# A hybrid decoder step on one core: small remainders of the experts as float32 blocks on four column groups, with earlier first weights and spread loads

## The chip, the cores and the metric

One core of a Trainium2 chip runs the whole step. The metric is the device time of one execution in microseconds; the kernel before takes 2387.33 us, the median of 3 runs.

## What is computed

One decoder layer over 2048 prompt rows and 8 decode rows, float32 throughout, width 1024. The last part is a mixture of experts: each row picks one of 4 groups and 2 of the 8 experts in it, so 2056 rows make 4112 assignments over 32 experts. Cut to what matters here:

```python
s = einsum(q, k) + bias            # three dilations (1, 4, 16), window 128 keys each, softmax, combined
x = x + gt1 * (concat([att, conv]) @ w_out)
h = rmsnorm(x, g_n2) * (1 + sc2) + sh2
eid, wts = route(h)                # group by argmax, then top 2 of its 8 experts
y[row] = sum over its 2 experts of wts * ((silu(h @ w1[e]) * (h @ w3[e])) @ w2[e])
x = x + gt2 * y                    # then one last rmsnorm
```

w1 (gate) and w3 (up) are 1024x512, w2 (down) is 512x1024, for each of the 32 experts: 6 MiB an expert.

## The kernel before

The step runs as stages one after another, each with its own buffers and with a barrier of all engines between them: setup and input projection; prompt attention; the decode rows' mixers; output projection and routing; experts; combining and the last norm. Engines are ordered by semaphores written out by hand; each engine runs its own program in its own order.

**Attention** (`prompt_attention`) walks 48 blocks of 128 queries: 16 for dilation 1, 16 for dilation 4, 16 for dilation 16. A block sees its own keys and mostly the block before (a wide block), or its own alone (narrow: all of dilation 16, and the first of each residue). SP loads at the start the bias bands of all three branches (lines 849 to 855), then QN, KN and VN (256 KB each) for the blocks to come (line 881 on), two slots for QN and KN. VectorE first waits for all three bias loads. ScalarE issues between its exponentials the loads for the stage behind: dec_q (2 MiB) at block 0, the three of dec_k (2 MiB each) at blocks 0 to 2, the three of dec_v at 12 to 14 (lines 1021 to 1029).

**Routing** (`output_projection_and_routing`) works tile by tile on 16 tiles of 128 rows and the decode rows: projection, norm, h2 stored to DRAM, router, rank of each row in its expert. POOL scatters each row's number into slot_tokens at expert x CAP + rank (line 1639). Counts of rows per expert come last, from one matmul and a VectorE copy.

**Experts** (`experts`, line 2040 on). `tables` (VectorE, lines 2096 to 2104) makes for each expert its number of 128-row blocks (at least one) and the first and the end of its run of blocks. Each engine reads these bounds into registers and loops over experts and blocks. For a block b of expert e:

- POOL loads 128 indices (IDX, line 2177) and gathers the rows (XG, line 2165), one block ahead: it waits until TensorE has transposed the block before (x_turned), then for its own gather.
- TensorE transposes XG into XP (line 2298). ScalarE rounds it to the fast float32r format (XH), VectorE takes the rest (XL).
- The weights are split likewise: ScalarE writes HI (line 2210, two halves a weight), VectorE LO (line 2256). A product is then three passes of float32r matmuls: HI with XH, HI with XL, LO with XH. Gate gives AE, up gives BE, 24 matmuls of 512 columns each (line 2309); ScalarE makes the silu SE from AE (line 2220), VectorE G = SE x BE in two halves (line 2267); TensorE turns G (line 2304), ScalarE and VectorE make GH and GL (lines 2224, 2271), and down gives YP, 24 matmuls (line 2314). ScalarE copies YP to YE in two halves (line 2230) and stores it (line 2232).
- In an expert's last block ScalarE and VectorE split the next expert's weights as well: gate after the silu, up after XH, down after the store (for VectorE all three after XL). SP loads a half of a raw weight (W1E, W3E, W2E; 1 MiB) as soon as VectorE has ended the same half of the expert before (lines 2149 to 2154).

`destinations` (VectorE, lines 2116 to 2120, in expert 0's first block) works out where each row's two results lie, for the last stage's gathers.

Of the kernel before, what the change touches and what calls it, by code (L numbers as in the profile page):

```python
# [9 lines left out]
F32R = mybir.dt.float32r  # L10
# [7 lines left out]
P = 128  # L18
# [26 lines left out]
MAXBLK = NEXP + (2 * ROWS) // P + 1  # L45
VEC = 384
# [71 lines left out]
def decoder_step(nc, t, const_at, stop_after=99):  # L118

    with ExitStack() as whole:  # L120
# [30 lines left out]
        with ExitStack() as both:  # L151
# [6 lines left out]
            if stop_after >= 3:  # L158
                decode_mixers(nc, t, scratch, const, const_at, state)
        if stop_after >= 4:  # L160
            state["token"] = persistent("token", [P, ALLT], I32)
            for name in ("rank", "expert", "weight"):
                state[name] = persistent(name, [P, ALLT, 2])
            state["count"] = persistent("count", [P, NEXP])
            state["lower"] = persistent("lower", [P, NEXP * NEXP])
            output_projection_and_routing(nc, t, scratch, const, const_at, state)
        late = whole.enter_context(ExitStack())
        if stop_after >= 5:
            for name, shape in (("gate6", [P, 2, D]), ("gf6", [P, D])):
                state[name] = persistent(name, shape)  # L170
            lasting = stage_semaphores(nc, late)
            state["mods6_in"] = lasting("mods6_in")
            state["blocks"] = persistent("blocks", [P, 2 * NEXP], I32)
# [567 lines left out]
def prompt_attention(nc, t, dr, const, state):  # L741
# [66 lines left out]
    with ExitStack() as ctx:  # L808
# [24 lines left out]
        bias_in = sem("bias_in")  # L833
# [12 lines left out]

        with nc.Block() as block:
            @block.sync
            def _(sp):
                for b in range(3):  # L850

                    v = dr["band"][b]
                    wide = 2 if b < 2 else 1
                    skew = bass.AP(v.tensor, v.offset + P - 1 + (2 - wide) * P, [[HEADS * VEC - 1, P], [VEC, HEADS], [1, wide * P]])
                    sp.dma_start(BIAS[b][:], skew).then_inc(bias_in, 16)

# [47 lines left out]
                for q in range(2):  # L904
                    load_qk(0, q, 0, None)
                step(0, 0)
# [31 lines left out]
            def _(dve):  # L938
                dve.wait_ge(bias_in, 48)
# [31 lines left out]
                def round_(g):  # L971
                    maxima(g)
                    if g.at or not g.fixed:
                        take_probs(g, 1)
                        take_columns(g, 1)

# [6 lines left out]
            def _(act):  # L983
# [37 lines left out]
                def ahead(g):  # L1021
                    dq_in, dk_in, dv_in = state["dec_in"]
                    if g == 0:
                        act.dma_start(state["dec_q"][:], dr["dec"][0:1].to_broadcast([P, DEC, DATT])).then_inc(dq_in, 16)
                    for at, cache, dst, come in ((0, t["cache_k"], state["dec_k"], dk_in), (3, t["cache_v"], state["dec_v"], dv_in)):
                        for n, dil in enumerate(DILATIONS):
                            if g == 4 * at + n:
# [429 lines left out]
def output_projection_and_routing(nc, t, dr, const, const_at, state):  # L1457
# [27 lines left out]
    with ExitStack() as ctx:  # L1485
# [9 lines left out]
        WO, WOH, WOL = sb("WO", [P, KD, D]), sb("WO_H", [P, KD, D], F32R), sb("WO_L", [P, KD, D], F32R)  # L1495
# [19 lines left out]
        NOROWS = sb("NOROWS", [P, D])  # L1515
        norows_set, norows_out, lower_in = sem("norows_set"), sem("norows_out"), sem("lower_in")
# [18 lines left out]
        with nc.Block() as block:  # L1535
            @block.sync
            def _(sp):
# [10 lines left out]

                def round_(i):
# [209 lines left out]
            def _(dve):  # L1759
# [141 lines left out]

                dve.wait_ge(mods_in, 16 * 11)
# [47 lines left out]
                nc.vector.tensor_copy(state["count"][:], NP_[:]).then_inc(count_ready, 1)  # L1950

# [98 lines left out]
def experts(nc, t, dr, const, state):  # L2050
# [4 lines left out]

    with ExitStack() as ctx:
# [3 lines left out]
        def ps(name, shape):  # L2060
# [4 lines left out]
        W1, W3, W2 = sb("W1E", [P, KD, DEXP]), sb("W3E", [P, KD, DEXP]), sb("W2E", [P, KF, D])  # L2065
        fetching = sem("fetching")
        IDX, XG, XH, XL = sb("IDX", [P, 1], I32), sb("XG", [P, D]), sb("XH", [P, KD, P], F32R), sb("XL", [P, KD, P], F32R)
        S, G, GH, GL, Y = sb("SE", [P, DEXP]), sb("GE5", [P, DEXP]), sb("GH", [P, KF, P], F32R), sb("GL", [P, KF, P], F32R), sb("YE", [P, D])
        HI = [sb(f"HI{n}", [P, KD * DEXP], F32R) for n in range(3)]
# [5 lines left out]
        w1_in, w3_in, w2_in = ([sem(f"{x}_w_in{half}") for half in range(2)] for x in ("gate", "up", "down"))  # L2075
# [3 lines left out]
            sem("y_taken"), sem("yrows_out"))  # L2079
        table = state["blocks"]  # L2080
        CMP, NBLK, LOW, START, END = sb("CMP", [P, NEXP, 16]), sb("NBLK", [P, NEXP]), sb("LOW", [P, NEXP, NEXP]), sb("START", [P, NEXP]), sb("END", [P, NEXP])
        SEL, BASE = sb("SEL", [P, ALLT * 2, NEXP]), sb("BASE", [P, ALLT * 2])
        step, table_ready = sem("table_step"), sem("table_ready")

# [438 lines left out]
```

## Time and profile before

| | |
|---|---|
| runs (3) | 2387.33 us median, 2385.10 to 2388.75 |
| profiled execution | 2385.13 us, of which the span 2383.6 us |
| busy in the span | TensorE 86%, its weight loads 70%, VectorE 68%, ScalarE 48%, POOL 24% |
| attention's first load to decode's first | 582.1 to 958.3 us |
| experts' stage | from 1360.2 to about 2285 us |
| mean granted clock | 0.936 of full |

In the rows, PE is TensorE's matmuls and PEld its weight loads, DVE is VectorE, ACT ScalarE, POOL GpSimd, and SPq or ACTq a DMA issue on that engine's queue. L2309 is line 2309 of the kernel before. A float32 matmul is recorded twice, a float32r one once. "Idle" is the engine's idle time before the group, and behind the arrow stands what ended it. A clock of 1.00 is 2.4 GHz, 0.50 is 1.2 GHz.

### The profile page before, as it was taken

What the parts mean: (1) busy time and instruction counts of PE and PEld (TensorE: products, weight loads), DVE (VectorE), ACT (ScalarE), POOL (GpSimd) and SP (SyncE); (2) the same over time, 40 slices, a digit from 0 to 9 for tenths busy, and PEclk for the clock granted to TensorE, in tenths of its full rate; (3) what the DMA queues carried; (4) which work ended last, traced back from release to release, by engine and by line L of the source; (5) the groups of instructions that cost most, each with busy time, mean ns of one, the idle gap of its engine ahead of it and who ended that gap; (6) DMA issues with size and microseconds to landing.
All of it is one profiled execution on the core that took longest, in us unless ns stands there. A gap on an engine that the chain in (4) does not pass through costs nothing. (4 is left out here: it accounts for less than half of the span.)

```text
span 2383.6 us, 37684 instructions
## 1 busy us (share of the span) xinstructions
PE 2059.1 (86%) x12062; PEld 1671.2 (70%) x12063; DVE 1627.6 (68%) x3132; ACT 1154.4 (48%) x2115; POOL 560.6 (24%) x560
## 2 busy tenths in 40 slices
PE   5999999996999997539999489999999999999910
PEld 3788888885777775328888368888888888888810
DVE  2568888887666666739998558664635666467868
ACT  2311111122777786024444158665546666457833
POOL 1024444440111111203555210000000000000066
PEclk7999999998999999659999689999999999999965
DMA  8755555554855454855776269876655878677977
GB/s 270 260 209 194 195 194 194 197 196 136 287 183 187 134 169 126 285 197 191 255 256 234 73 243 397 319 279 257 242 198 198 330 271 303 235 260 294 380 280 294
DMA packets 221091, 560.26 MB, mean 235 GB/s; under 512 B 27885, under 2 KB 41541, under 8 KB 219848
## 3 DMA queue, kind: packets, MB, share of 16 engines
q1 hardware_dynamic: 178544, 436.70, 52.3%
q0 software_dynamic: 26144, 79.49, 9.1%
q10 hardware_dynamic: 16320, 43.01, 4.8%
q8 instruction: 46, 0.75, 0.1%
q14 instruction: 37, 0.30, 0.0%
HBM read 460.66 MB, written 171.04 MB: 265 GB/s over the span
## 5 line engine op out<-in xcount | busy, mean ns | idle before, releaser
L591 DVE SCALAR_TENSOR_TENSOR ARENA<-ARENA,TAPW 128x512 f32<-128x512 f32 (+3 forms) x493 | 293.3, 674 | 0.0
L417 POOL TENSOR_TENSOR MS<-SSQ,K 128x1 f32<-128x1 f32 x17 | 172.3, 10136 | 289.8 <-ACT H L460 289.8
L2267 DVE TENSOR_TENSOR GE<-SE,BE 128x256 f32<-128x256 f32 x98 | 36.9, 418 | 272.0 <-PE BE L2309 269.6
L710 PE MATMUL PJ<-WIN_H,HTH 128*128 128x512 f32 x680 | 172.4, 396 | 15.1 <-ACT HTH L466 11.7
L492 ACT ACTIVATE ARENA<-PJ 128x512 f32<-128x512 f32 x51 | 30.5, 600 | 293.6 <-PE PJ L718 293.6
L1017 ACT ACTIVATE PR<-SBX,NM 128x256 f32<-128x256 f32 (+1 forms) x384 | 171.9, 456 | 1.0 <-PE TB L1104 0.8
L714 PE MATMUL PJ<-WIN_H,HTL 128*128 128x512 f32 x680 | 170.4, 393 | 0.0
L718 PE MATMUL PJ<-WIN_L,HTH 128*128 128x512 f32 x680 | 168.1, 389 | 0.0
L710 PEld LDWEIGHTS PJ<-WIN_H,HTH 128*128 128x128 f32 x680 | 127.3, 189 | 45.8 <-ACT HTH L466 15.9
L2165 POOL DMA_INDIRECT XG<-h_rows,IDX x50 | 50.4, 1008 | 455.3 <-PE XP L2298 439.9
L714 PEld LDWEIGHTS PJ<-WIN_H,HTL 128*128 128x128 f32 x680 | 129.7, 191 | 27.4
L718 PEld LDWEIGHTS PJ<-WIN_L,HTH 128*128 128x128 f32 x680 | 127.6, 188 | 26.5
L2256 DVE TENSOR_TENSOR LO<-W1E,HI 128x2048 fp32r<-128x2048 f32 x64 | 143.6, 2283 | 3.4 <-ACT HI L2210 3.4
L2256 DVE TENSOR_TENSOR LO<-W3E,HI 128x2048 fp32r<-128x2048 f32 x64 | 143.6, 2284 | 0.6 <-ACT HI L2210 0.6
L2256 DVE TENSOR_TENSOR LO<-W2E,HI 128x2048 fp32r<-128x2048 f32 x64 | 143.6, 2285 | 0.0
L2210 ACT CAST HI<-W1E 128x2048 fp32r<-128x2048 f32 x64 | 120.1, 1902 | 36.2 <-DMA W1E<-in_w_expert_gate 35.7
L952 DVE CUSTOM_DVE_ANT_0 SBX<-S,BIAS 128x256 f32<-128x256 f32 (+1 forms) x384 | 117.5, 362 | 22.7 <-issue 22.7
L2210 ACT CAST HI<-W2E 128x2048 fp32r<-128x2048 f32 x64 | 120.5, 1911 | 25.6 <-ACT YE L2230 14.9
L2210 ACT CAST HI<-W3E 128x2048 fp32r<-128x2048 f32 x64 | 120.1, 1918 | 1.7 <-DMA W3E<-in_w_expert_up 1.5
L2177 POOL DMA_DIRECT2D IDX<-slot_tokens x48 | 27.5, 573 | 355.8 <-issue 245.0
L2314 PE MATMUL YP<-HI,GH 128*128 128x512 f32 x392 | 104.6, 409 | 4.2 <-ACT GH L2224 3.2
L1127 PE MATMUL OT<-PTS,VN 128*64 128x128 f32 x1200 | 90.8, 284 | 19.2 <-DVE PTS L965 19.2
(310 smaller groups left out, 4717.7 us busy)
## 6 DMA issues: line engine op xcount, KB each, us to landing
W1E<-in_w_expert_gate SPq DMA_DIRECT2D x64, 1024.0 KB, 8.3
W3E<-in_w_expert_up SPq DMA_DIRECT2D x64, 1024.0 KB
W2E<-in_w_expert_down SPq DMA_DIRECT2D x64, 1024.0 KB, 11.6
expert_rows<-YE ACTq DMA_DIRECT2D x49, 512.0 KB, 5.8
expert_rows<-NOROWS POOLq DMA_DIRECT2D x11, 1536.0 KB, 11.7
WAD<-in_w_ada SPq DMA_DIRECT2D x16, 1024.0 KB, 7.0
X<-in_x_prompt SPq DMA_DIRECT2D x31, 512.0 KB
QN<-q_rows SPq DMA_DIRECT2D x48, 256.0 KB, 3.1
```

Source lines behind the costliest of these rows:

```text
L417: pool.tensor_tensor(MS[:], SSQ[:], const("eps"), ALU.add).then_inc(ms_ready, 1)
L591: ins = nc.vector.scalar_tensor_tensor(out=out, in0=src, scalar=tap, in1=out, op0=ALU.mult, op1=ALU.add)
L710: nc.tensor.matmul(PJ[:, n], HTH[:, k], WH[:, n, k], start=k == 0, stop=False)
L714: nc.tensor.matmul(PJ[:, n], HTL[:, k], WH[:, n, k], start=False, stop=False)
L718: mm = nc.tensor.matmul(PJ[:, n], HTH[:, k], WL[:, n, k], start=False, stop=k == KD - 1)
L952: nc.vector.tensor_tensor_reduce(SBX[hh][:, h, 0:wide], SP_[hh][:, at_bank(h), 0:wide], bias, 1.0, -3e38, ALU.add, ALU.max, ml[:, head:hea ...
L1017: ins = nc.scalar.activation(PR[hh][:, h, 0:w], SBX[hh][:, h, 0:w], ACT.Exp, bias=NM[:, head:head + 1], scale=1.0, accum_out=ML[g.q][:, HE ...
L1127: mm = nc.tensor.matmul(OT[s * DH:(s + 1) * DH, pair], VN[(q - nk + 1 + k) % 4][:, head * DH:(head + 1) * DH], PTS[:, u, n], start=k == 0, ...
L2165: pool.indirect_dma_start(XG[:], None, dr["h2"], bass.IndirectOffsetOnAxis(ap=IDX[:].bitcast(U32), axis=0)).then_inc(x_in, 16)
L2210: nc.scalar.copy(HI[n][:, cols], raw[n][:, cols]).then_inc(hi_ready[n], 1)
L2256: nc.vector.tensor_tensor(LO[n][:, cols], raw[n][:, cols], HI[n][:, cols], ALU.subtract).then_inc(lo_ready[n], 1)
L2314: mm = nc.tensor.matmul(YP[:, half * 512:half * 512 + 512], g[:, k], w[2][:, k * D + half * 512:k * D + half * 512 + 512], start=first and ...
```

## The change

**Experts.** The first of an expert's rows may form a small block of up to 32 rows (`SMALL_ROWS`), when count - 128 x FULL is 1 to 32, where FULL is the number of full blocks, at least one; such an expert has one full block less than before. Experts 0 and 31 always have a small block. The 32 experts become runs that begin with a small block. A small block uses the raw float32 weights: its rows are the stationary operand, 32 columns wide, and a weight's columns go in four quarters to four groups of 32 rows of the output.

**First weights.** W1E and W3E share a buffer (WIDE) with the projection's raw w_out, and expert 0's gate and up are requested in the routing stage's last rounds; its down is requested after the first gather. The table is made at the end of the routing stage; the destinations are worked out at the end of VectorE's program in the experts' stage.

**Attention.** QN and KN go first, then the first branch's bias; ScalarE issues the other two at blocks 1 and 2. dec_k goes out at blocks 3, 13 and 15, dec_v at 32, 34 and 44, dec_q at 46.

The diff, cut to its core:

```diff
+SMALL_ROWS = 32
 # attention
-                dve.wait_ge(bias_in, 48)
+                dve.wait_ge(bias_in[0], 16)
...
                 for q in range(2):
                     load_qk(0, q, 0, None)
+                load_bias(sp, 0)
...
+                    if g in (1, 2):
+                        load_bias(act, g)
-                    if g == 0:
+                    if g == 46:
                         act.dma_start(state["dec_q"][:], ...)
 # routing: last rounds of SP
+                def first_expert(name, n):
+                    sp.wait_ge(w_lo_ready, KD)
...
+                    if isinstance(i, int) and i == TILES - 2:
+                        first_expert("w_expert_gate", 0)
+                    if isinstance(i, int) and i == TILES - 1:
+                        first_expert("w_expert_up", 1)
 # routing: VectorE, after the counts (each operation waits for the one before)
+                def experts_table(dve):
+                    then(nc.vector.tensor_scalar(FULL[:], count[:], 1.0 / P, (P - T - 0.5) / P - 0.5, ALU.mult, ALU.add))
+                    then(nc.vector.tensor_scalar(FULL[:], FULL[:], 8388608.0, None, ALU.add))
+                    then(nc.vector.tensor_scalar(FULL[:], FULL[:], -8388608.0, 1.0, ALU.add, ALU.max))
+                    then(stt(SMALL1[:], FULL[:], float(P), count[:], ALU.mult, ALU.is_lt))
+                    for e in (0, NEXP - 1):
+                        then(nc.vector.tensor_scalar(SMALL1[:, e:e + 1], SMALL1[:, e:e + 1], 1.0, None, ALU.max))
+                    below(RUN, SMALL1)
+                    below(FROM, FULL)
...
 # experts: SP
+                sp.wait_ge(x_in, 16)
+                for half in range(2):
+                    sp.dma_start(half_of(W2[:], half), half_of(w2[0], half)).then_inc(w2_in[half], 16)
                 with sp.Fori(1, NEXP) as e:
                     split = sp.snap(e * 2)
+                    sp.wait_ge(sy_done, entry(sp, 4, e, 1, LAST))
...
 # experts: POOL
+                def fetch_small(e, n):
+                    pool.wait_ge(sx_turned, n + 1)
+                    pool.dma_start(IDXS[:], dr["slot"][ds(slot, T), :]).then_inc(sidx_in, 16)
+                    pool.wait_ge(sidx_in, n * 16 + 16)
+                    pool.indirect_dma_start(XGS[:], None, dr["h2"], ...).then_inc(sx_in, 16)
...
+                with pool.Fori(0, number) as g:
+                    head, behind = run(pool, g)
+                    fetch_small(behind, g + 1)
+                    with pool.Fori(pool.snap(head + 1), pool.snap(behind + 1)) as e:
+                        ...
 # experts: ScalarE
+                def small(e, n, meanwhile=None):
+                    act.wait_ge(sx_turned, n + 2)
+                    nc.scalar.copy(XS[:], XPS).then_inc(sx_ready, 1)
+                    act.wait_ge(sa_done, n + 1)
+                    nc.scalar.activation(SS[:], APS, ACT.Silu).then_inc(ss_ready, 1)
+                    act.wait_ge(sg_turned, n + 1)
+                    nc.scalar.copy(GTS[:].rearrange("p k t -> p (k t)"), GPS).then_inc(sgt_ready, 1)
+                    act.wait_ge(sy_out, n * 64 + 64)
+                    act.wait_ge(sy_done, n + 1)
+                    nc.scalar.copy(YS[:], YPS).then_inc(sy_taken, 1)
+                    for q in range(4):
+                        act.dma_start(dr["y"][ds(row, T), cols], YS[q * T:(q + 1) * T]).then_inc(sy_out, 16)
...
+                    with act.Fori(head, behind) as e:
+                        upper(2, e)
+                        first, last = first_and_last(act, e)
...
+                        block_(last, g + 1, lambda n: upper(n, e + 1))
+                    small(behind, g + 1)
 # experts: VectorE has the same loops
+                def small(n):
+                    dve.wait_ge(ss_ready, n + 1)
+                    dve.wait_ge(sb_done, n + 1)
+                    nc.vector.tensor_tensor(GS[:], SS[:], BPS, ALU.mult).then_inc(sg_ready, 1)
 # experts: TensorE
+                def on_groups(out, x, w, ks):
+                    width = w.shape[2] // 4
+                    for k in range(ks):
+                        for q in range(4):
+                            mm = nc.tensor.matmul(out[q * T:(q + 1) * T], x[:, k], w[:, k, q * width:(q + 1) * width], start=k == 0, stop=k == ks - 1)
+                def small(e, n, meanwhile=None):
+                    pe.wait_ge(sx_in, n * 16 + 16)
+                    for k in range(KD):
+                        mm = nc.tensor.transpose(XPS[:, k], XGS[:, k * P:(k + 1) * P], const("ident")[0:T, 0:T])
+                    pe.wait_ge(sx_ready, n + 1)
+                    on_groups(APS, XS, W1, KD).then_inc(sa_done, 1)
+                    on_groups(BPS, XS, W3, KD).then_inc(sb_done, 1)
+                    pe.wait_ge(sg_ready, n + 1)
+                    nc.tensor.transpose(GPS, GS[:], const("ident")).then_inc(sg_turned, 1)
+                    pe.wait_ge(sgt_ready, n + 1)
+                    on_groups(YPS, GTS, W2[:], KF).then_inc(sy_done, 1)
```

In the loops over a run's experts upper(0) and upper(1) of the next expert (ScalarE) and lower(0), lower(1) (VectorE) stay in an expert's last block; upper(2) and lower(2) stand at the start of the expert itself, behind a small block where there is one. TensorE's small block waits for both halves of each raw weight.

## Rows read from the trace of the kernel before

In a row of a stretch the engines stand in the order PE, PEld, DVE, ACT, POOL (busy us and instructions), then the granted clock, the DMA engines' busy share and GB/s; with one line alone, PE and PEld only.

**Rows 1.** Busy time by engine in the experts' stage: window, length, engines, granted clock, DMA, GB/s.

```profile
1360.00:2285.00 925.00, 888.44 (x4124) 728.40 (x4124) 570.47 (x450) 583.27 (x535) 83.78 (x105) 0.98 0.74 277
```

**Rows 2.** The page's groups (busy, mean ns, idle, releaser) and its DMA issues.

```profile
L2267 DVE TENSOR_TENSOR GE<-SE,BE 128x256 f32<-128x256 f32 x98 | 36.9, 418 | 272.0 <-PE BE L2309 269.6
...
expert_rows<-YE ACTq DMA_DIRECT2D x49, 512.0 KB, 5.8
```

**Rows 3.** Timeline of TensorE: start, length; the first group of each block.

```profile
1403.69 1.98 PE L2309 MATMUL AE<-HI,XH 128*128 128x512 f32 x8
1421.72 1.98 PE L2309 MATMUL AE<-HI,XH 128*128 128x512 f32 x8
...
1513.49 1.98 PE L2309 MATMUL AE<-HI,XH 128*128 128x512 f32 x8
```

**Rows 4.** Timeline of ScalarE and VectorE at a handover, and the copies GH by line.

```profile
1421.92 0.59 ACT L2230 COPY YE<-YP 128x512 f32<-128x512 f32 x1 [0.27 <-PE YP L2314]
...
1423.03 4.49 DVE L2256 TENSOR_TENSOR LO<-W3E,HI 128x2048 fp32r<-128x2048 f32 x2
1423.08 3.73 ACT L2210 CAST HI<-W2E 128x2048 fp32r<-128x2048 f32 x2 [0.57 <-ACT YE L2230]
...
L2224 ACT CAST GH<-GP 128x256 fp32r<-128x256 f32 x86 | 31.5, 372 | 121.9 <-PE GP L2304 119.3
```

**Rows 5.** Line 1414 alone in two stretches (two clocks), and line 1448 in the timeline.

```profile
971.30:975.20 3.90, 3.64 (x64) 2.98 (x64) 0.50 0.75 117
978.20:979.60 1.40, 1.08 (x32) 0.81 (x32) 1.00 0.88 322
...
1003.79 5.36 PE L1448 MATMUL OD<-dec_v,PTD 128*32 128x512 f32 x48
```

**Rows 6.** Timeline of TensorE's weight loads in attention.

```profile
646.81 0.42 PEld L1127 LDWEIGHTS OT<-PTS,VN 128*64 128x64 f32 x8 [0.17 <-issue]
```

**Rows 7.** Timeline of POOL in one block, and DMA issues with median time to landing.

```profile
1416.73 0.98 POOL L2165 DMA_INDIRECT XG<-h_rows,IDX  x1 [10.30 <-PE XP L2298]
1423.60 0.57 POOL L2177 DMA_DIRECT2D IDX<-slot_tokens  x1 [5.89 <-issue]
...
W1E<-in_w_expert_gate SPq DMA_DIRECT2D x64, 1024.0 KB, 8.3
...
IDX<-slot_tokens POOLq DMA_DIRECT2D x49, 0.5 KB, 4.9
```

**Rows 8.** Timeline over the end of routing and expert 0's first block.

```profile
1353.29 0.85 POOL L1639 DMA_INDIRECT slot_tokens<-TOK,SLOTP  x1 [0.30 <-issue]
...
1360.29 0.69 DVE L2096 TENSOR_TENSOR CMP<-count,K 128x512 f32<-128x512 f32 x1 [10.47 <-PEq L191]
...
1361.95 1.23 DVE L2100 TENSOR_TENSOR LOW<-lower,NBLK 128x1024 f32<-128x1024 f32 x1
...
1378.51 3.75 PE L2309 MATMUL AE<-HI,XH 128*128 128x512 f32 x8 [1.10 <-ACT XH L2204]
...
1396.04 0.69 PE L2304 MATMUL GP<-K,GE 128*128 128x128 f32 x2 [3.40 <-DVE GE L2267]
...
1397.24 2.98 PE L2314 MATMUL YP<-HI,GH 128*128 128x512 f32 x8
```

**Rows 9.** Timeline at attention's start, QN's landing there, and one QN slot later.

```profile
582.14 2.61 SPq L855 DMA_DIRECT2D BIAS<-band_rows  x3
...
593.17 1.12 PE L1060 MATMUL XPA<-K,QN 128*128 128x128 f32 x4 [20.76 <-DMA QN<-q_rows]
...
597.80 0.06 DVE L948 MEMSET PAUSE<- 128x1 f32 x1 [18.62 <-PE S L1089]
...
QN<-q_rows SPq DMA_DIRECT2D x3, 256.0 KB, 6.7
...
888.69 0.33 SPq L881 DMA_DIRECT2D QN<-q_rows  x1
...
898.97 0.32 PE L1060 MATMUL XPA<-K,QN 128*128 128x128 f32 x1
```

More of the change, by code:

```diff
@@ L159, in decoder_step @@
                 decode_mixers(nc, t, scratch, const, const_at, state)
+        late = whole.enter_context(ExitStack())
         if stop_after >= 4:
+            state["wide"] = persistent("WIDE", [P, KD * D])
+            lasting = stage_semaphores(nc, late)
+            state["first_in"] = [[lasting(f"{x}_w_in{half}") for half in range(2)] for x in ("gate", "up")]
             state["token"] = persistent("token", [P, ALLT], I32)
@@ L2130, in first_and_last, with runs, run @@
             return first, engine.snap(end - 1)
-        raw = [w[:].rearrange("p k n -> p (k n)") for w in (W1, W3, W2)]
+        def runs(engine):
+            return entry(engine, 4, LAST, 1, LAST)
+        def run(engine, g):
+            return entry(engine, 0, g, 0, LAST - 1), entry(engine, 0, g + 1, 1, LAST)
+        raw = [w.rearrange("p k n -> p (k n)") for w in (W1, W3, W2[:])]
         come = (w1_in, w3_in, w2_in)
@@ L2161, in _, with place @@
             def _(pool):
+                def place(value, rows):
+                    return nc.s_assert_within(pool.snap(value), 0, NEXP * CAP - rows,
+                                              skip_runtime_bounds_check_because="an expert's blocks stay inside its CAP slots")
                 def gather(b):
@@ L2316, in into_rows @@
                     return mm
-                pe.wait_ge(table_ready, 1)
-                pe.wait_ge(x_in, 16)
-                turn_x(range(KD)).then_inc(x_turned, 1)
-                with pe.Fori(0, NEXP) as e:
+                def on_groups(out, x, w, ks):
+                    width = w.shape[2] // 4
+                    for k in range(ks):
+                        for q in range(4):
+                            mm = nc.tensor.matmul(out[q * T:(q + 1) * T], x[:, k], w[:, k, q * width:(q + 1) * width],
+                                                  start=k == 0, stop=k == ks - 1)
+                    return mm
@@ L2359, in combine_and_normalise, with first_rows @@
+                def first_rows():
+                    pe.wait_ge(x_in, 16)
+                    turn_x(range(KD)).then_inc(x_turned, 1)
+                small(0, 0, first_rows)
+                number = runs(pe)
+                with pe.Fori(0, number) as g:
+                    head, behind = run(pe, g)
+                    with pe.Fori(head, behind) as e:
+                        expert(e, g + 1)
+                    small(behind, g + 1)
+                expert(LAST, number + 1)
 def combine_and_normalise(nc, t, dr, const, state):
```

320 lines of the change are left out of this document (197 added, 123 removed).

## The prediction

> **What bounds the kernel now.** I read the stretches of the stages first, then the page's costliest groups, then the timeline where one expert's block hands over to the next. In the experts' stage TensorE is busy 888 of 925 us at a clock of 0.98 of full [rows 1], and VectorE stands 272 us before the product that follows BE, released by TensorE [rows 2]: the stage is as long as TensorE's list of blocks. The timeline gives the price of a block: 1403.69 to 1421.72 is 18.03 us, and 1421.72 to 1513.49 is five blocks of experts with one block each, 18.35 us a block [rows 3]; the 0.3 us more is a weak pull of the weights' loads (6 MiB for each expert). The page stores 49 blocks [rows 2]. So a removed block is worth 18.0 us, and what is added between two blocks costs in full what TensorE cannot overlap.
>
> How many blocks go is in the inputs. The reference's own router on its inputs gives the 32 experts 141, 101, 85, 64, 72, 120, 134, 183, 89, 212, 168, 139, 141, 348, 138, 107, 83, 208, 134, 111, 74, 135, 143, 242, 167, 130, 59, 123, 83, 50, 62 and 66 rows. Rounded up to 128 that is 49 blocks, as the trace has. By the new rule (a remainder of 1 to 32 rows is small) 40 full blocks are left: experts 0, 6, 11, 12, 14, 18, 21, 22 and 25 lose one each. Ten small blocks run: these nine, and one without rows for expert 31, which the code forces.
>
> **A small block, step by step**, on the handover at 1421.5, where TensorE begins the weight loads of the next AE (0.2 ahead of the row at 1421.72).
> - Eight transposes of 32 rows: 1.0 us, to 1422.6. Their rows were gathered long before.
> - ScalarE copies them out (XS). It is in order behind YE (ends 1422.5) and the store, and came free at 1423.08 [rows 4]; a 128x256 copy from PSUM takes 0.37 [rows 4], so TensorE resumes at 1423.6.
> - Gate and up: per weight 32 matmuls of 128x32 weights by 128 columns in float32, in four column groups, each recorded twice. That very shape is in the trace: 32 records in 1.08 us at full clock, 64 in 3.64 at half clock [rows 5]. So 64 records take about 1.9, two weights 3.7: to 1427.3. The silu and its table load lie beside the second.
> - The product on VectorE: that engine is in LO of W3E from 1423.03 for 4.49, to 1427.5 [rows 4]. A tie with the matmuls. A 128x128 product is under the 0.42 of 128x256 [rows 2]; I take 0.3: 1427.9.
> - Transpose, copy to GTS, semaphores: 0.7, to 1428.6.
> - Down: 16 matmuls of 256 columns. The nearest row is 24 of 512 columns in the same groups, 5.36 us [rows 5], so 16/24 x 1/2 of it: 1.8, to 1430.4.
>
> That is 8.9 us. The PE array changes between full width and groups four times. **The row**: between full-width and 64-column matmuls the weight loads pause 0.17 us [rows 6]; two of the four changes lie beside a wait, so 0.3. The Trainium skill (TensorEngine Tiling (Array Packing), Key Properties) says that changing the tiling mode drains the engine. By a full drain of some 0.27 us at each of four changes, an estimate from that page and this kernel's matmul length, ten small blocks would cost 8 us more than I count; the row says less, and I go by the row. I add 0.8 for register loads, loop ends and branches on three engines, which no row shows by themselves (bounds 0 and 3), and 0.5 for the next gather (first rival). **A small block costs 10.5 us**, between 8.9 and 14.
>
> ScalarE then stores four pieces (some 0.4 each) and splits W2E, 3.7 [rows 4], to about 1436.5, VectorE ends its LO by 1441; the full block that began at 1430.7 wants them at 1443.5. Covered; without that cover each small block would cost up to 2.5 more. Eight experts (6 to 25 above) thus give 8 x (18.0 - 10.5) = 60.2 us, expert 31 costs 10.5.
>
> **Expert 0 and the stage's start.** Before: stage start 1360.3, expert 1 at 1421.7, 61.4 us, of which the first block took 25 (1378.51 to 1403.69) because its G came late from VectorE, which was at LO of W2E and the destinations (3.4 us of idle TensorE), and then ran its YP at a lower clock (2.98 us for eight) [rows 8]. After, counted from the start: small index load (4.9 to land [rows 7]) and gather, 12; index and gather of the 128 rows behind them, 20 (a gather lands 6.9 after its issue [rows 7]); only then is W2E requested, and its second half lands some 8.3 later [rows 7], 28.3, so that is what the small block's last matmuls wait for; then 2 us and one full block of 18: 48.9. Gain 12.5. Against it, the table moves ahead of the barrier, into the tail of the routing stage, and grows: 7 operations of 128x1024 at 1.23 and some 14 of 32 columns or fewer, which by the line through 0.69 (512 columns) and 1.23 (1024) take about 0.2 with their semaphore, 11.7 us [rows 8]. VectorE ended at 1360.29 - 10.47 = 1349.8 and would now end at 1361.5, while the barrier followed the last scatter (1353.29, landed some 3 later) by about 3. The start moves from 1360.3 to 1364.7, **4.4 us later**. Net 8.1. The early loads of gate and up are 4 MiB on SP behind that stage's last x2 and h2 traffic; SP has nothing late behind them, cost 0. The destinations, four operations, move to VectorE's end, beside the last YP, its copy and store: 0, and a few us if they outlast those.
>
> **Attention.** SP issued the three BIAS loads first at 582.14, the first transposes came at 593.17, released by QN, and VectorE started at 597.80, 18.6 idle [rows 9]. With QN and KN ahead, TensorE starts some 6 earlier; BIAS of branch 0 lands around 592, just when the scores are done. I take 5.5 (bounds 3 and 7). The spread loads: beside them a QN took 6.7 to land [rows 9], but a QN slot is loaded at 888.69 and used again two short blocks on, at 898.97 [rows 9]: slack 10, cost 0. The last one, dec_q at block 46, ends some 8 us before the next stage starts; bound 2.
>
> **Sum**: 60.2 - 10.5 + 8.1 + 5.5 = 63.3 off the profiled execution's 2385.1 (span 2383.6, 1.5 around it) is 2321.8. The median of the runs is 2387.3, 2.2 above that execution: **2324**.
>
> **Rivals.**
> - *The gather becomes the wait.* POOL now fetches the next small block's rows (index, wait, gather) before the next full block's index and gather. From the small transposes at 1422.7: 4.9 + 1 + 0.5 + 4.9 + 1, and 6.9 to land: 1441.9, and TensorE wants it some 11 us into the block, 1441.7. A tie; I counted 0.5. If index loads land 1 us later each, beside three weights in flight, 2 us more at eight experts: 2340. Chance 0.2.
> - *Weights too late.* SP waits for the small block before it requests the next expert's weights, all at once at 1430.4, where they went out from 1421 on. W1E's second half lands at 1438.7, and ScalarE splits it before it copies GH, wanted at 1442.6. It fits by 2 us; if the landing is 12, some 5 us at eight experts: 2364. Chance 0.1.
> - *Slower: the small block runs at half clock.* The place is the holes of 1.0, 0.6 and 0.5 us inside it. The trace has the fall: after 3.4 us without work the next eight matmuls took 2.98 for 1.98 [rows 8]. At half clock gate and up take 7.3 for 3.7, down 3.6 for 1.8, transposes 1.1 more, the block behind 1.4 more: 18.1 for each small block, and 2392 in all. It decides from 17.5 us per small block (63.3 / 9 above 10.5). Against it: around 978 TensorE worked 1.08 us of a 1.40 us stretch on this very shape, and the granted clock there was 1.00 [rows 5]. Chance 0.04. The Trainium skill (TensorE: Matmul & The Clock Gate, What's actually happening) has activity release the throttle and idleness bring it back; that fits this row.
> - *The groups run one after another here*: 3.4 and 1.8 become four times as much, 24 us per small block: 2445. The rows of that shape speak against it. Chance 0.02.
> - *Cheaper than counted*: 9 us per small block, a shorter start: 2306. Chance 0.1. That the blocks do not go is excluded by the counts, unless the rule is not what I read: 0.01.
>
> **Numbers.** Forecast 2324 with 0.53, own range 2310 to 2336. 8 in 10 reaches over the gather's case and the first part of the weights' case: 2302 to 2356. A measurement here tells 0.2%, 5 us, from no change. Faster 0.93, same 0.02 (half clock in part), slower 0.05.
>
> **What would show it.** Forty stores of YE and ten of each small tile; full blocks 18.0 apart, 28.5 where a small one lies between. In a small block: TensorE idle before gate on ScalarE's copy, before the transpose on VectorE's product, with LO of W3E ended just before. Expert 1 starting 49 us into the stage, the stage's start at 1359 (4.4 later, 5.5 earlier), VectorE's first maximum near 592. Wrong if idle time before the XG transposes exceeds 1 us per small expert, if eight matmuls behind a small block take over 2.5, or if gate and up take more than 5.

## The result, and the profile after

The changed kernel takes 2371.23 us (median of 6 runs, 2364.32 to 2377.85), the kernel before on the same chip 2388.04 (6 runs). The ratio is 0.9931, 95% interval 0.9913 to 0.9950: faster by 17 us, where 63 were forecast. 2324 was predicted, and the range ended at 2356. The profiled execution took 2364.32 us, its span 2362.8.

The blocks go as forecast. These are issues on the page of the changed kernel (tile, queue, count, KB each, median us to landing), against 49 in [rows 2]; each small block stores four pieces of YS:

```profile
expert_rows<-YE ACTq DMA_DIRECT2D x40, 512.0 KB, 5.3
...
expert_rows<-YS ACTq DMA_DIRECT2D x40, 32.0 KB
```

And yet the run of blocks got no shorter. Busy time by engine from the first matmul of expert 1's block to that of the last block, in the kernel before and then in the changed one (columns as in [rows 1]):

```profile
1421.72:2254.82 833.10, 828.95 (x3865) 680.20 (x3864) 525.70 (x411) 547.45 (x502) 70.91 (x91) 1.00 0.76 283
```

```profile
1399.37:2233.88 834.51, 778.95 (x4714) 621.22 (x4713) 511.75 (x382) 471.78 (x445) 79.94 (x92) 0.98 0.75 279
```

Eight full blocks fewer lie in this stretch and nine small ones more. It lasts 1.4 us longer, and TensorE, busy 829 of 833 us before, now stands 56 us. All that the change gained lies outside it. By the two traces: attention begins 4.1 us earlier (the setup before it is the same code; over this study's traces the start moved between 577.6 and 583.3), attention and the decode stage are 8.3 shorter from their first load to the projection's first matmul, projection and routing are 4.9 longer, the stretch from the experts' first index load to expert 1 is 14.9 shorter. That sums to 4.1 + 8.3 - 4.9 + 14.9 - 1.4 = 21.0, and the two profiled executions differ by 20.8. Two of these terms are larger in this pair than on the mean. The changed kernel's profiled execution is the fastest of its six. And the stretch from attention's first load to the projection took 474.5 to 477.7 us in the three traces with the old attention code, and 469.4 to 475.8 in the eleven with the new one, of which this is the shortest.

Two things fill the stretch. **First, full blocks are slower where nothing waits.** TensorE's timeline (start, length), one group of eight matmuls to the next, first before:

```profile
1657.85 1.98 PE L2309 MATMUL AE<-HI,XH 128*128 128x512 f32 x8
1659.66 1.98 PE L2309 MATMUL AE<-HI,XL 128*128 128x512 f32 x8
...
1668.74 0.82 PE L2298 MATMUL XP<-K,XG 128*128 128x128 f32 x6
...
1670.31 2.12 PE L2314 MATMUL YP<-HI,GH 128*128 128x512 f32 x8
```

and after:

```profile
1564.98 2.03 PE L2440 MATMUL AE<-HI,XH 128*128 128x512 f32 x8
1566.85 2.03 PE L2440 MATMUL AE<-HI,XL 128*128 128x512 f32 x8
...
1576.18 0.82 PE L2429 MATMUL XP<-K,XG 128*128 128x128 f32 x6
...
1577.92 2.09 PE L2445 MATMUL YP<-HI,GH 128*128 128x512 f32 x8
...
1583.59 2.03 PE L2440 MATMUL AE<-HI,XH 128*128 128x512 f32 x8
```

Eight wide matmuls (128x128 weights by 512 columns) take 1.87 us and not 1.81, and from the XG transposes to YP it is 1.74 and not 1.57. A block takes 18.61 us (1564.98 to 1583.59) against 18.04. **Second, a small block costs 13.5 us** on the mean of the eight inside the loop, not 10.5. (This is the time from the AE of the full block ahead of it to the AE behind it, less one full block of 18.61.) The one at expert 6, TensorE and then ScalarE:

```profile
1493.63 2.02 PE L2445 MATMUL YP<-LO,GH 128*128 128x512 f32 x8
1495.58 0.68 PE L2466 MATMUL XP<-K,XGS 32*128 32x32 f32 x8
1498.29 3.32 PE L2454 MATMUL AE<-WIDE,XS 128*32 128x128 f32 x64 [2.03 <-ACT XS L2312]
1501.44 1.93 PE L2454 MATMUL BE<-WIDE,XS 128*32 128x128 f32 x64
1503.94 0.30 PE L2483 MATMUL GP<-K,GS 128*128 128x128 f32 x1 [0.58 <-DVE GS L2383]
1504.68 1.93 PE L2454 MATMUL YP<-W2E,GTS 128*32 128x256 f32 x32 [0.45 <-ACT GTS L2318]
1509.06 2.12 PE L2440 MATMUL AE<-HI,XH 128*128 128x512 f32 x8 [2.44 <-issue]
```

```profile
1497.79 0.37 ACT L2312 COPY XS<-XP 128x256 f32<-128x256 f32 x1 [1.52 <-issue]
```

The products come out as worked out (1.77 for gate at full clock and 1.93 for down; the sum had 1.9 and 1.8). What is above it are three things. XS is copied 1.5 us after the copy of YE ended, where the sum had 0.6 for the store between them. Gate ran 3.15 us instead of 1.77. And 2.4 us pass between the small block's last matmul and AE.

### The profile page after: what moved, and what is told of

The parts are those of the page before. It is cut to its first block and busy times, and to the rows that moved or that the text cites. A ratio compares the mean times of both kernels' runs of the same rounds, so it can differ in the third digit from the quotient of the medians.

```text
span 2362.8 us, 40338 instructions
## 1 busy us (share of the span) xinstructions
PE 1990.6 (84%) x12996; PEld 1597.2 (68%) x12997; DVE 1612.0 (68%) x3110; ACT 1074.3 (45%) x2054; POOL 568.7 (24%) x562
## 5 line engine op out<-in xcount | busy, mean ns | idle before, releaser
L2374 DVE TENSOR_TENSOR LO<-WIDE,HI 128x2048 fp32r<-128x2048 f32 x128 | 284.5, 2283 | 15.5 <-ACT HI L2303 15.5
L2303 ACT CAST HI<-WIDE 128x2048 fp32r<-128x2048 f32 x128 | 240.1, 1908 | 55.0 <-DMA WIDE<-in_w_expert_gate 33.1
L715 PEld LDWEIGHTS PJ<-WIN_H,HTH 128*128 128x128 f32 x680 | 127.2, 189 | 46.1 <-ACT HTH L471 15.9
L2390 DVE TENSOR_TENSOR GE<-SE,BE 128x256 f32<-128x256 f32 x80 | 30.0, 416 | 180.8 <-PE BE L2440 180.8
L2440 PE MATMUL AE<-HI,XH 128*128 128x512 f32 x320 | 89.4, 425 | 20.9 <-issue 20.9
L1115 PE MATMUL TB<-K,PR 128*128 128x128 f32 x600 | 85.3, 278 | 9.7 <-ACT PTS L1013 8.3
L926 POOL DMA_DIRECT2D branch_rows<-O x48 | 25.9, 540 | 279.9 <-ACT O L1007 279.9
L2440 PEld LDWEIGHTS AE<-HI,XH 128*128 128x128 f32 x320 | 64.4, 204 | 41.2 <-issue 26.0
```

Of the source, the lines that this page charges most:

```text
L715: nc.tensor.matmul(PJ[:, n], HTH[:, k], WH[:, n, k], start=k == 0, stop=False)
L1115: mm = nc.tensor.transpose(TB[u % 2][:, n], PR[head // HH][:, head % HH, k * P:(k + 1) * P], const("ident"))
L2303: nc.scalar.copy(HI[n][:, cols], raw[n][:, cols]).then_inc(hi_ready[n], 1)
L2374: nc.vector.tensor_tensor(LO[n][:, cols], raw[n][:, cols], HI[n][:, cols], ALU.subtract).then_inc(lo_ready[n], 1)
L2440: mm = nc.tensor.matmul(out, x[:, k], w[n][:, k * DEXP:(k + 1) * DEXP], start=first and k == 0, stop=last and k == KD - 1)
```

## The experiments

**1, 2. Where the matmuls lose 3%.** The buffers of the change move everything that is allocated behind them. In the built kernels HI and LO begin at a multiple of 64 bytes in a partition before, and 32 bytes off one after. Both ways round:

```
+        sb("SHIM", [P, 8])
         HI = [sb(f"HI{n}", [P, KD * DEXP], F32R) for n in range(3)]
```

> The changed kernel with one 32-byte buffer put ahead of HI0, so that HI0 to HI2 and LO0 to LO2 begin at a multiple of 64 bytes in a partition, as before the change; nothing else differs. Theory A (the start of the weights' halves in SBUF sets the pace of the wide matmuls): the full block comes back from 18.60 to 18.03 us, eight matmuls from 1.87 to 1.81 us, and the time falls by 40 x 0.57 = 22.8 us, to about 2348. Theory B (the slower pace is contention with the more spread transfers, or the added waits): nothing moves, 2371.

> The kernel before with the same 32-byte buffer ahead of HI0, which here moves HI and LO off the multiple of 64 bytes. Theory A: the block goes from 18.03 to 18.60 us and the time rises by 49 x 0.57 = 28 us, to about 2416. Theory B: 2388, no change.

Measured: the first 2357.85 us, 0.9883 [0.9867, 0.9898], a gain of 11 us on the changed kernel's 0.9931; the second 2404.55, 1.0075 [1.0061, 1.0089], 18 us lost by a buffer that nothing uses. The second's matmuls take 1.87 us for eight, as in the changed kernel. So the place of the operands is a cause, and theory B falls as it was put. But both moved less than theory A said, 11 us for 23 and 18 for 28. In the second a block takes 18.48 and not 18.60, so the place is worth 0.44 us of the 0.57, and something else the rest. And the first stopped at 1.83 and a block of 18.31, so a multiple of 64 is not the whole rule.

**3. Without small blocks.**

```
-(P - T - 0.5) / P - 0.5
+(P - 0.5) / P - 0.5
```

> The changed kernel with its table rounding every remainder up to a full block, so that only the two forced small blocks (experts 0 and 31) are left and eight small blocks become full ones. Theory A (a small block costs 13.5 us as the trace of after shows it, and nothing beside it): 8 x (18.6 - 13.5) = 41 us slower than the changed kernel, about 2412. Theory B (the small blocks also cost the blocks around them, the sum of their gain being nearer to nothing): less than 20 us slower. Theory C (the price of the prediction, 10.5, and the loss lies elsewhere): 65 us slower, 2436.

2421.51 us, 1.0150 [1.0132, 1.0168]: 50 us slower than the changed kernel. My arithmetic missed that expert 0 gets a second full block too: nine full ones come, eight small ones go. 9 x 18.6 - 50 = 117, or 14.7 us for each small block, in line with 13.5 and the 0.6 of the block behind it in the trace. The small blocks do gain, some 4 us each against an equally slow full block.

**4. Attention alone**, in the kernel before (with the spread of dec_k and dec_v as in the change):

```
-for b in range(3):
-    sp.dma_start(BIAS[b][:], skew).then_inc(bias_in, 16)
 for q in range(2):
     load_qk(0, q, 0, None)
+load_bias(sp, 0)
...
-dve.wait_ge(bias_in, 48)
+dve.wait_ge(bias_in[0], 16)
```

> The kernel before with the attention part of the change alone (first band and first loads ahead of the other two bands, dec loads at later blocks). By the prediction's step: 5.5 us faster, 2382.5. Rival: the gain is the 11 us by which the decode stage starts earlier in the trace of after, 2377. Second rival: the moved loads cost it back later, 2388.

2382.32 us (9 runs), 0.9979 [0.9968, 0.9990]: 5.0 us. The step of 5.5 holds. In its trace VectorE starts 6.6 us earlier than in [rows 9] (591.18 for 597.80), and the projection's first matmul comes 3.6 earlier (1056.3 for 1059.9).

**5, 9. Which property of the place.** A 96-byte buffer instead of 32, then one of 480:

```
-        sb("SHIM", [P, 8])
+        sb("SHIM", [P, 24])
...
+        sb("SHIM", [P, 120])
```

> The changed kernel with a 96-byte buffer ahead of HI0, so that HI and LO begin at 64 modulo 128 bytes, as before the change and as XH and GH do (with the 32-byte buffer of the first run they began at 0 modulo 128). There eight matmuls took 1.83 us against 1.814 before. Theory A (the place within 128 bytes counts too): 1.814 us, block 18.31 to 18.17, 5 us faster than the first run, about 2352. Theory B (a multiple of 64 is all that counts, the 0.016 us is something else): 2358, block 18.31.

2361.13 us, 0.9888 [0.9871, 0.9905], block 18.55: both theories fail. HI is at a multiple of 64, at the phase within 128 bytes that it had before, and the pace is back at 1.86. What was left was the distance to the stationary operand.

> The changed kernel with a 480-byte buffer ahead of HI0. HI, LO, XH, XL, GH and GL then all begin at 448 modulo 512 bytes, so that a matmul's weight tile (512 bytes a slice) and its moving rows (2048 bytes) have one phase. The phases so far, moving start less stationary start modulo 512, and eight matmuls: 0 (kernel before, experts) 1.814 us, 64 (first run) 1.83, 128 (the 96-byte run) 1.86, 32 (kernel before shifted, and the changed kernel) 1.867. Theory A (the difference of the two starts sets the pace): 1.814 us, block 18.18 with the 0.15 us of waits around the transposes, about 2354, 17 us faster than the changed kernel. Theory B (the moving rows' own start counts: 0 modulo 2048 was the better one in the first run): 1.83 or slower, block 18.3 or more.

2354.44 us, 0.9861 [0.9846, 0.9877]. TensorE's timeline of the 96-byte run, then of the 480-byte run:

```profile
1575.80 2.02 PE L2441 MATMUL AE<-HI,XH 128*128 128x512 f32 x8
1577.66 2.03 PE L2441 MATMUL AE<-HI,XL 128*128 128x512 f32 x8
```

```profile
1568.06 1.98 PE L2441 MATMUL AE<-HI,XH 128*128 128x512 f32 x8
1569.88 1.98 PE L2441 MATMUL AE<-HI,XL 128*128 128x512 f32 x8
1571.69 1.98 PE L2441 MATMUL AE<-LO,XH 128*128 128x512 f32 x8
```

With both operands at one phase (the same start modulo 512 bytes) eight matmuls take 1.81 us again, and the block 18.18: theory A. The total falls 17 us below the changed kernel, but only 7 below the 96-byte run, where 38 blocks x 0.37 would be 14. In its trace the nine small blocks cost 118.7 us for 113.9 and the blocks behind them lose 5.6 for 3.8, both with more of them at half clock; the other full blocks lose 9.0 for 5.1, mostly among the experts with one block each, where the weights' loads set the pace (last section).

**10. The same in another stage, in the kernel before:**

```
+        sb("SHIM3", [P, 120])
         MIX, MTH, MTL = ...
```

> The kernel before with a 480-byte buffer ahead of MT_H in the output projection's stage, so that MT_H, MT_L, WO_H and WO_L all begin at 0 modulo 512 bytes (MT_H and MT_L were at 32). 816 wide matmuls. Theory A (difference of starts): eight of them go from 1.867 to 1.814 us, 102 groups x 0.053 = 5.4 us faster, 2382. Theory B: 2387.5, no change.

2385.48 us (12 runs), 0.9999 [0.9990, 1.0007]: the pace follows, the time does not. From one tile's first group to the next tile's, in the kernel before and then here:

```profile
1154.99 2.10 PE L1987 MATMUL OP<-WO_H,MT_H 128*128 128x512 f32 x8
1156.93 2.03 PE L1987 MATMUL OP<-WO_H,MT_L 128*128 128x512 f32 x8
1158.80 2.03 PE L1987 MATMUL OP<-WO_L,MT_H 128*128 128x512 f32 x8
...
1168.37 1.06 PE L1976 MATMUL TPS<-K,MIX 128*128 128x128 f32 x8 [0.24 <-issue]
...
1170.97 2.10 PE L1987 MATMUL OP<-WO_H,MT_H 128*128 128x512 f32 x8
```

```profile
1152.27 2.09 PE L1988 MATMUL OP<-WO_H,MT_H 128*128 128x512 f32 x8
...
1156.01 1.98 PE L1988 MATMUL OP<-WO_L,MT_H 128*128 128x512 f32 x8
1157.83 1.98 PE L1988 MATMUL OP<-WO_H,MT_H 128*128 128x512 f32 x8
1159.64 1.98 PE L1988 MATMUL OP<-WO_H,MT_L 128*128 128x512 f32 x8
...
1165.66 1.07 PE L1977 MATMUL TPS<-K,MIX 128*128 128x128 f32 x8 [0.52 <-issue]
...
1168.27 2.09 PE L1988 MATMUL OP<-WO_H,MT_H 128*128 128x512 f32 x8
```

Groups are 1.81 apart for 1.87, yet a tile still takes 16.0 us (1152.27 to 1168.27 here, 1154.99 to 1170.97 before): TensorE stands 0.52 us instead of 0.24 ahead of the TPS transposes. So something else sets this stage's pace. Which engine or transfer it is was not looked for, and I had costed the stage by TensorE alone.

**6. The added wait.**

```
+pe.wait_ge(hi_ready[2], e * 2 + 2)
+pe.wait_ge(y_taken, b * 2 + 2)
+pe.wait_ge(sy_taken, n + 1)
 pe.wait_ge(x_in, b * 16 + 32)
 turn_x(range(6))
...
 turn_g(1)
-pe.wait_ge(hi_ready[2], e * 2 + 2)
-pe.wait_ge(y_taken, b * 2 + 2)
-pe.wait_ge(sy_taken, n + 1)
 pe.wait_ge(gh_ready, b * 2 + 3)
```

> As the run with the 96-byte buffer, but TensorE's three waits ahead of the down product (W2's upper half, y_taken and the new sy_taken) stand ahead of the transposes of XG, behind which 1.8 us of matmuls are queued. Theory A (the added wait on a register's value is the 0.10 us by which YP starts later after GH is there, 1.74 instead of 1.57 us behind the XP transposes): block shorter by 0.10, 4 us faster in all. Theory B (the later start is all the 0.08 us by which GE and GH start later): no change.

2363.52 us, 0.9899 [0.9882, 0.9916] against the 96-byte run's 0.9888: the medians cannot tell. The trace can: YP starts 1.64 us behind the XP transposes (1580.03 to 1581.67) and not 1.74, and a block takes 18.49 for 18.55. The effect is real, some 0.07 us a block or 3 in all, and is drowned by the scatter of the small blocks' clock. Of the 0.17 by which YP came later than before, 0.10 goes with the place of these waits; the other 0.07 was not settled. But the edit moved three waits, two of which the kernel before has as well, so it does not show that the new one alone costs the 0.10.

**7. The hole ahead of AE.** TensorE's loop is turned:

```
 mm.then_inc(sx_turned, 1)
+known = ahead()   # bounds of this expert, end of the run
 for half in range(2):
     pe.wait_ge(w1_in[half], e * 16 + 16)
...
-with pe.Fori(0, number) as g:
-    head, behind = run(pe, g)
-    with pe.Fori(head, behind) as e:
-        expert(e, g + 1)
-    small(behind, g + 1)
+known = small(head, g, ahead=...)
+from_small(head, g, known, after)
```

> As the run with the 96-byte buffer, but on TensorE the loop is turned so that a small block's own expert's first and last block and the next run's end are loaded behind the small block's transposes, where TensorE waits for XS, instead of between the small block's last matmul and the next full block. Theory A (the hole of 2.35 us ahead of AE, which expert 31 outside the loop has at 0.31, is loads of registers and loop turns): the hole falls to about 0.6 us in nine small blocks, 15 us faster in all. Theory B (the hole is the cost of a jump, such as fetching instructions that were not run last): the hole stays at 2 us or more, no gain or a few us lost, since the code is longer.

2348.59 us, 0.9846 [0.9833, 0.9858]: 10 us below the 96-byte run by the ratios (12.5 by the medians). The same small block without the hole:

```profile
1783.97 1.93 PE L2455 MATMUL YP<-W2E,GTS 128*32 128x256 f32 x32 [0.45 <-ACT GTS L2319]
1785.84 2.13 PE L2441 MATMUL AE<-HI,XH 128*128 128x512 f32 x8
```

AE follows at once in all nine cases, so the hole was the seam between the loops, though 10 us came where the holes summed to 19. Loads at the top of the loop now lengthen the wait for XS from 2.0 to 2.2 us, and seven of nine gates ran slow, where three had. The run does not tell theory A from a cost of the jump itself. In the changed kernel the jump back of the outer loop stands at the seam too, and the turned loop moves it behind a full block's long matmuls, together with the loads. That expert 31's seam, with two of the four loads and no jump back, had 0.31 us speaks for the jump or the other two loads, and leaves open which.

**8. The hole ahead of gate.**

```
-row = 0 if isinstance(e, int) else out_row(entry(act, 1, e, 0, MAXBLK) * P + n * T, T)
 act.wait_ge(sx_turned, n + 2)
 nc.scalar.copy(XS[:], XPS).then_inc(sx_ready, 1)
+row = 0 if isinstance(e, int) else out_row(entry(act, 1, e, 0, MAXBLK) * P + n * T, T)
```

> As the run with the 96-byte buffer, but ScalarE loads and checks the small block's output row behind the copy to XS and not ahead of it. Theory A (the 1.5 us that ScalarE stands idle ahead of XS, put down to issue, is this load with its loop turn): the copy starts about 0.8 us earlier, 9 x 0.8 = 7 us faster in all. Theory B (the loop turn alone takes it): no change.

2355.05 us, 0.9871 [0.9855, 0.9888], 4 us below the 96-byte run (6 by the medians), with theory A at 0.65 us for each:

```profile
1779.51 1.96 PE L2455 MATMUL AE<-WIDE,XS 128*32 128x128 f32 x64 [1.35 <-ACT XS L2312]
1781.28 1.94 PE L2455 MATMUL BE<-WIDE,XS 128*32 128x128 f32 x64
```

**The clock, over all the traces with small blocks.** Half clock was a rival of the prediction, and its rate can be counted. The slow gate of the changed kernel stands at 0.54, near the lower level of 1.2 GHz, what follows at 2.4. The granted clock (last but two) of a slow gate in the changed kernel, the up product right behind it, and a gate of the run just above:

```profile
1498.40:1501.40 3.00, 3.00 (x64) 2.87 (x68) 2.52 (x2) 0.00 (x0) 0.84 (x1) 0.54 0.13 38
1501.60:1503.20 1.60, 1.60 (x67) 1.49 (x56) 0.00 (x0) 0.28 (x1) 0.07 (x1) 1.00 0.30 82
```

```profile
1779.60:1781.20 1.60, 1.60 (x64) 1.60 (x68) 1.60 (x2) 0.00 (x0) 0.00 (x0) 1.00 0.60 233
```

Gates that took over 2 us (expert 0's left out): with TensorE idle 1.34 to 1.38 us before gate 1 of 10; 1.6 us (eight gates of the run below) 2 of 8; 2.0 us (eight kernels) 27 of 56; 2.2 to 2.3 us 6 of 8. For AE behind the hole of 2.35 us it was 26 of 56, and with none, or the 0.3 us of expert 31, 0 of 26. So slow products are more frequent here behind longer holes, and none of these lengths makes one certain. Below 1.6 us the counts are small, and the one slow gate there (3.52 us behind 1.38 us idle) shows that a short hole is no guarantee. A slow gate, with what of up is slow behind it, costs 1.4 to 1.7 us, a slow AE 1.0 to 1.6.

**11. All of it together:** the edits of the ninth, tenth (here ahead of the changed kernel's MT_H), sixth, seventh and eighth run.

> The changed kernel with all that was tried: one phase in the experts' stage and in the projection, TensorE's bounds loaded inside the small block, its three waits ahead of the XG transposes, the small block's copy ahead of its output row's load. If the terms add: 2371 - 17 (phase) - 4 (waits) - 5 (projection) - 15 (bounds) - 7 (copy) = about 2323, which is the 2324 of the prediction. Rival: they overlap in the stretches that wait for weights and for the clock, and a third is lost: 2340.

**2327.81 us, 0.9742 [0.9720, 0.9764]**: 59 us faster than the kernel before, between the two expectations and nearer to the first. A small block inside the loop costs 10.1 us, a full block 18.11:

```profile
1767.15 0.68 PE L2470 MATMUL XP<-K,XGS 32*128 32x32 f32 x8
1769.43 1.95 PE L2456 MATMUL AE<-WIDE,XS 128*32 128x128 f32 x64 [1.60 <-ACT XS L2313]
1771.19 1.94 PE L2456 MATMUL BE<-WIDE,XS 128*32 128x128 f32 x64
1773.69 0.30 PE L2488 MATMUL GP<-K,GS 128*128 128x128 f32 x1 [0.57 <-DVE GS L2385]
1774.44 1.93 PE L2456 MATMUL YP<-W2E,GTS 128*32 128x256 f32 x32 [0.45 <-ACT GTS L2320]
1776.31 2.14 PE L2442 MATMUL AE<-HI,XH 128*128 128x512 f32 x8
```

**12. The first expert's weights asked for late.**

```
-if isinstance(i, int) and i == TILES - 2:
-    first_expert("w_expert_gate", 0)
-if isinstance(i, int) and i == TILES - 1:
-    first_expert("w_expert_up", 1)
...
+for dst, src, come in weights[:2]:
+    for half in range(2):
+        sp.dma_start(half_of(dst, half), half_of(src[0], half)).then_inc(come[half], 16)
 sp.wait_ge(x_in, 16)
```

> The changed kernel with the first expert's gate and up weights asked for at the start of the experts' stage, as W2's are close behind, and not in the routing stage. From the trace of after: the 4.2 MB would land about 11 to 12 us behind the stage's start, the gate product of expert 0 starts about 4 us later than the 8.8 us it has now, and the down product, which in after waits 5.95 us for W2E, still waits for W2E, since that is asked for at XG's arrival in both. Theory A (W2E is the wait of expert 0, so the early load hides behind it): expert 1's block starts 0 to 2 us later, time 2371 to 2373. Theory B (the prediction's step, where the early load carries the start's gain of 12.5 us less the forced block): 8 us slower or more, 2379.

2372.77 us, 0.9951 [0.9935, 0.9966], against 0.9931 [0.9913, 0.9950]: unclear. The traces say more: from the first index load to expert 1's AE it is 46.1 us in the changed kernel (1353.28 to 1399.37) and 52.8 here (1357.78 to 1410.57). Down waits for W2E in both, as theory A has it, but W2E is asked for behind two gathers, and these now stand behind the weights:

```profile
1364.41 2.14 POOL L2261 DMA_INDIRECT XGS<-h_rows,IDXS  x1 [6.03 <-DMA IDXS<-slot_tokens]
...
1370.94 1.03 PE L2465 MATMUL XP<-K,XGS 32*128 32x32 f32 x8 [28.26 <-DMA XGS<-h_rows,IDXS]
```

In the changed kernel the index took 2.24 us to land, and the transposes ran 3.14 us behind the gather's issue; here 6.03 and 6.53. The early load is worth up to 7 us in this stretch, by a way that neither theory named. The other seven traces with small blocks and the early load have 44.6 to 47.8 us there, so the 52.8 stands out, while the times are too close to tell.

## Why the prediction was wrong, by its own steps

**Sum.** From expert 1 to the last block the prediction's prices give 38 full blocks x 18.04 + 9 small x 10.5 + the 3.3 us that before loses to late weights = 783 us. The trace has 834.5, 51 more:
- *Full blocks at 18.0, as before*: 38 x 0.57 = **21.7**. This is the step that failed without being a step: I priced what the change adds and removes, and took the price of what stays from [rows 3] with no bound. 0.43 a block is the operands' phase (shown by the second and the ninth run), 0.07 goes with the place of the three waits ahead of the down product (sixth run), 0.07 is open.
- *Small block 10.5*: 119.6 for nine instead of 94.5, **25.1**. This is the second step that failed, by its size. Of the 8.9 us that the rows gave, the matmuls, the product and the transposes held. The three inside the loop whose gate ran at full clock took 12.1 to 12.2: these 8.9 and the first of the following terms, little else. Three terms were mis-sized. "0.8 for register loads, loop ends and branches", with bounds 0 and 3, was 3.0, at its upper bound: 2.35 on TensorE alone, ahead of AE, behind a down product of 1.93 us (the seventh run takes it away), and 0.65 on ScalarE ahead of XS (eighth run). Half clock was priced as all or nothing (18.1 us, chance 0.04); it came to six of nine gates and four AE, at 1.4 to 1.7 us each. The 0.5 for the gather was not needed: XGS and XG were there.
- *The block behind a small one*: **5.0**, mostly slow AE, which the prediction had in a rival alone. Less 0.6 for other blocks: 51.2.

Of these 51 us the profiled execution shows 42.5 in its total (2364.3 for 2321.8): the setup, attention and the start came out some 9 us better than their terms, in part by the luck of this pair. The medians miss by 47. Two of the prediction's three signs of being wrong are in the trace: eight matmuls behind a small block took 3.4 us and more in four cases (sign: 2.5), and gate and up together 5.1 to 5.4 in six (sign: 5).

**Blocks removed**: right, 49 to 40 and ten small ones.

**The start**: right in its sum, in part by luck. 48.9 us were forecast from the stage's start to expert 1; by index loads, it is 46.1 against 60.9 before, a gain of 14.9 for 12.5. W2E is the small block's last wait, as forecast, but it ends 20 us into the stage and not 28, since the index loads and gathers land sooner than in [rows 7] (2.24 us for the first index, 4.9 counted). Then the down product ran at half clock, a hole of 1.67 us followed, and the full block took 20.6 us, where 2 and 18 were counted:

```profile
1373.44 3.64 PE L2454 MATMUL YP<-W2E,GTS 128*32 128x256 f32 x32 [5.95 <-DMA W2E<-in_w_expert_down]
1378.74 3.46 PE L2440 MATMUL AE<-HI,XH 128*128 128x512 f32 x8 [1.67 <-issue]
```

The table made routing longer by 4.9 us between the projection's first matmul and the stage's first index load (300.9 to 305.8), forecast 4.4.

**Attention**: right, 5.0 (2.4 to 7.6) for 5.5, by the fourth run.

**Rivals.** The gather and the late weights did not come, nor groups one after another. The slower end asked for 17.5 us a small block; 14 with the block behind it, and 0.57 on every full block, took away 47 of the 63 us, three quarters of the way to no gain at all. The Trainium skill's rule on tiling (TensorEngine Tiling (Array Packing), Key Properties), a drain at each change of mode, was priced by its estimate at 0.27 us a change; the trace leaves room for about 0.1. With the bounds loaded early, full-width AE starts 1.87 us behind the start of a down product that is 1.93 long, an overlap of 0.06, where gate and up in one mode overlap by 0.18 (1.77 apart, 1.95 long). Going the other way, the small transposes start 1.91 us behind the last eight wide matmuls, and another eight wide ones 1.81 (both in the eleventh run). Its other rule, that idleness brings the throttle back (TensorE: Matmul & The Clock Gate, What's actually happening), was cited beside a row that spoke against half clock here. The runs bear the rule out (half clock behind 2.35 us of idleness in 26 of 56 cases, behind 0.3 us or less in none of 26), and that row's stretch of 1.40 us had 0.32 us idle in it, less than the small block's 2.0.

The forecast itself is met, to 4 us, by the kernel that takes these terms away (2327.81 for 2324). That is part luck too: its run of blocks takes 794.8 us and not 783, for late weights and slow gates, and the start gives 4 us of that back (44.6 for 48.9). So the missing terms are these, and the agreement to 4 us is not a measure of how well the rest was sized.

## What to carry to other kernels

Price what stays as well: a change that allocates buffers moves all those behind it, so compare the operands' starts in the build and one untouched group of matmuls in the trace before reading anything else. The loads and the turn of two nested loops cost nothing here behind a full block's matmuls and 2.35 us behind a small block's, so load the next bounds while the engine waits for data, and put the jump back behind long work, not at the seam. Where holes can tip the clock, price them by a rate and not as a rival that is on or off, and expect the runs to scatter: 14 us over six runs of the changed kernel, 5 over those before beside it.

## What the runs showed of the hardware

**The phase of the two operands.** float32r matmuls of 128x128 by 512 columns, eight of them: 1.81 us where the moving and the stationary operand begin at the same place modulo 512 bytes of a partition (both at 448 in the experts' stage before and in the ninth run, both at 0 in the tenth), 1.83 at a difference of 64, 1.86 at 128, 1.87 at 32 (the changed kernel, the second run, and the projection of both kernels, where it is the stationary operand that lies 32 further). That is 227 and 233 ns each. The moving operand's start alone does not set it: at 0 modulo 512 it goes with 1.83 in the first run (stationary at 448) and with 1.81 in the tenth (stationary at 0). Other differences, whether the neighbours' traffic matters, and whether the period is 512 bytes or 256, were not tried.

**A ceiling that moves.** Where experts have one block each, the DMA engines are busy throughout, and faster blocks mostly wait for weights. The kernel before, then the eleventh run, in such a stretch:

```profile
1460.00:1480.00 20.00, 19.74 (x93) 16.19 (x92) 17.63 (x13) 17.23 (x14) 1.56 (x2) 1.00 1.04 397
```

```profile
2130.00:2150.00 20.00, 18.50 (x88) 15.12 (x86) 16.36 (x12) 14.62 (x13) 3.66 (x3) 1.00 1.03 379
```

The rate is 396 to 398 GB/s throughout such stretches before, at a busy share of 1.04, and 379 to 393 in the last version, at 1.03 (down to 361, where the share falls to 0.98). Blocks there take 18.6 to 21.7 us, some 12 us in all above 18.11; in the longest, ScalarE stands 3.60 us for a half of the gate weights:

```profile
2161.80 1.90 ACT L2305 CAST HI<-WIDE 128x2048 fp32r<-128x2048 f32 x1 [3.60 <-DMA WIDE<-in_w_expert_gate]
```

Why the rate is lower was not tried, and stays open.
